# The output linear of the mixer: two of its four pairs as one unit of seven products, with another order of fetches and small work

## The reference, cut to what matters

```python
merged = jax.nn.sigmoid(ga) * (ya @ w_proj_a[l]) + jax.nn.sigmoid(gb) * (yb @ w_proj_b[l])
h = h + gt2[:, None, :] * (merged @ w_out[l])

u = modulate(rmsnorm(h, g_ff2[l]), sh3, sc3)
h = h + FFN_RES * gt3[:, None, :] * swiglu(u, w2_gate[l], w2_up[l], w2_down[l])
```

## Time and profile before

| what | us |
|---|---|
| median of 3 runs (lowest to highest) | 1180.81 (1180.71 to 1181.24) |
| the profiled execution | 1179.22 |
| its span in the trace | 1177.4 |
| TensorE (PE) busy in it | 1164.3 |
| VectorE (DVE) busy | 737.2 |
| ScalarE (ACT) busy | 352.1 |
| GpSimd (POOL) busy | 86.2 |

### The profile page before, as it was taken

One profiled execution on the slowest core, in us unless ns is written; L12 is line 12 of the kernel. 1 busy time (PEld: TensorE's weight loads), 2 busy tenths in 40 slices (PEclk: granted clock), 3 DMA queues, 4 the chain that ended last, 5 costly groups with the idle time before them and its releaser, 6 DMA issues.

```text
span 1177.4 us, 21319 instructions
## 1 busy us (share of the span) xinstructions
PE 1164.3 (99%) x8862; PEld 1076.8 (91%) x8862; DVE 737.2 (63%) x1658; ACT 352.1 (30%) x996; POOL 86.2 (7%) x104
## 2 busy tenths in 40 slices
PE   9999999999999999999999999999999999999997
PEld 7889999998878999999999999988888998888887
DVE  4558888675148866982898888567845231167632
ACT  2111210232124555212321210245333431056542
POOL 0000000200011000022000000310004010001111
PEclk9999999999999999999999999999999999999999
DMA  9969949762655457676599759574524643642311
GB/s 344 366 217 321 315 154 313 290 245 90 219 180 187 150 214 259 236 264 231 185 342 304 235 201 294 193 260 171 146 61 144 215 144 114 187 136 73 117 63 36
DMA packets 164272, 241.78 MB, mean 205 GB/s; under 512 B 14033, under 2 KB 112559, under 8 KB 164176
## 3 DMA queue, kind: packets, MB, share of 16 engines
q1 hardware_dynamic: 156256, 230.45, 57.9%
q10 hardware_dynamic: 6784, 5.74, 1.7%
q0 software_dynamic: 1136, 4.22, 1.1%
HBM read 236.82 MB, written 4.62 MB: 205 GB/s over the span
## 4 chain that ended last, share of the span: by engine, by line
PE 91%; DVE 5%; DMA 2%; ACT 1%; issue 1%; POOL 0%; DVEq 0%; ACTq 0%
PE ps L189 89%; PE ps L192 2%; DVE arena L198 2%; DMA slots<-in_w_proj_a 1%; DVE x L198 1%; DMA slots<-in_w_proj_b 1%; ACT U L195 1%; DVE slots L207 1%; ACT tmps L195 0%; DVE arena L204 0%; DVE rstd L216 0%; DVE tmps L204 0%; DVE slots L198 0%; DVE tmps L198 0%; POOL arena L198 0%
## 5 line engine op out<-in xcount | busy, mean ns | idle before, releaser
L189 PE MATMUL ps<-U,slots 128*128 128x128 f32 (+2 forms) x2800 | 478.7, 330 | 0.0
L189 PEld LDWEIGHTS ps<-U,slots 128*128 128x128 f32 (+1 forms) x2800 | 419.7, 190 | 40.7 <-issue 4.7
L189 PE MATMUL ps<-arena,slots 128*128 128x128 f32 (+1 forms) x1776 | 237.6, 294 | 0.0
L189 PEld LDWEIGHTS ps<-arena,slots 128*128 128x128 f32 x1776 | 225.3, 192 | 8.6 <-issue 0.4
L195 ACT ACTIVATE tmps<-ps 128x256 f32<-128x256 f32 (+2 forms) x151 | 57.4, 383 | 343.4 <-PE ps L189 319.4
L207 DVE CUSTOM_DVE_ANT_0 arena<-arena,tmpA 128x1024 f32<-128x1024 f32 x96 | 118.2, 1275 | 19.3 <-DMA arena<-in_w_adaT 19.1
L195 ACT ACTIVATE arena<-ps 128x256 f32<-128x256 f32 (+3 forms) x150 | 59.5, 416 | 155.9 <-PE ps L189 152.1
L189 PE MATMUL ps<-arena 128*128 128x128 f32 (+7 forms) x940 | 101.9, 287 | 0.9 <-DVE arena L198 0.9
L189 PEld LDWEIGHTS ps<-arena 128*128 128x128 f32 (+2 forms) x940 | 92.4, 181 | 9.8 <-issue 4.2
L189 PE MATMUL ps<-ABT,arena 128*128 128x128 f32 (+5 forms) x752 | 81.9, 271 | 0.0
L189 PEld LDWEIGHTS ps<-ABT,arena 128*128 128x128 f32 (+3 forms) x752 | 72.5, 174 | 0.8 <-issue 0.8
(11 more groups left out here) (199 smaller groups left out, 1140.6 us busy)
## 6 DMA issues: line engine op xcount, KB each, us to landing
slots<-in_w_in SPq DMA_DIRECT2D x14, 2048.0 KB, 10.3
slots<-in_w_down SPq DMA_DIRECT2D x16, 1408.0 KB, 9.8
slots<-in_w_gate SPq DMA_DIRECT2D x18, 1024.0 KB, 8.0
slots<-in_w_up SPq DMA_DIRECT2D x18, 1024.0 KB, 10.8
arena<-in_w_adaT SPq DMA_DIRECT2D x36, 512.0 KB, 6.1
arena<-in_ada_w1T SPq DMA_DIRECT2D x24, 512.0 KB, 7.5
slots<-in_a_in_w SPq DMA_DIRECT2D x6, 2048.0 KB, 9.8
slots<-in_b_in_w SPq DMA_DIRECT2D x12, 1024.0 KB, 5.4
```

What stands on the lines that cost most here:

```text
L189: return Nothing() if self.e is None else self.e.matmul(*a, **k)
```

## The change

The output linear's block 0 (pairs 0 and 1) becomes the fourteenth entry of `U7`, with `GA` as its source, and stands between the first halves of pairs 2 and 3. Each "ada" transfer is fetched behind the two blocks of weights that it stood ahead of, and wo 0 ahead of ada 17. The pieces of ada are moved to other j by a table, the last four behind the loop: two behind the first residual of pair 2, two behind that of pair 3, and mod 17 behind those. The third sums t3 of ("pa", 0) and ("pb", 0) go behind `v_s7` of their source. The residual of block 0 is taken from SBUF in four instructions.

```diff
             for n, g in (("ga", 13), ("gb", 14), ("op", 15), ("pa", 16), ("pb", 17)):
-                fetch("ada", g)
                 fetch(n, 0)
                 fetch(n, 1)
-            fetch("wo", 0)
+                if n == "pb":
+                    fetch("wo", 0)
+                fetch("ada", g)
             fetch("wo", 1)
...
-        U7 = [("xm", 1), ("va", 0), ("va", 1)] + [(n, b) for n in ("ga", "gb", "op", "pa", "pb") for b in range(2)]
+        U7 = [("xm", 1), ("va", 0), ("va", 1)] + [(n, b) for n in ("ga", "gb", "op", "pa", "pb") for b in range(2)] + [("wo", 0)]
-        OF7 = {"pa": "ya", "pb": "hc"}
+        OF7 = {"pa": "ya", "pb": "hc", "wo": "mg"}
...
+            elif n == "wo":
+                x = two(arena[:, 11296:12320])
...
+        def source_in(tag, k):
+
+            return act.at("ya out", k // 2) if tag == "ya" else dve.at("yb", k) if tag == "hc" else pool.at("mg", k // 4, 0)
...
-            mg = lambda k, half: pool.at("mg", k // 4, 1)
-            for pair in range(4):
-                t_linear(e, "wo", pair, GA, mg, half=0 if pair >= 2 else None, side=pair == 0)
-                if pair == 1:
-                    for x in free_of(S3) + free_of(X2):
-                        e.wait_ge(*x)
+            mg = lambda k, half: pool.at("mg", k // 4, half)
+            t_linear(e, "wo", 2, GA, mg, half=0)
+            t_u7_first(e, 13)
+            t_u7_second(e, 13)
+            t_linear(e, "wo", 3, GA, mg, half=0)
+            for x in free_of(S3) + free_of(X2):
+                e.wait_ge(*x)
             t_linear(e, "wo", 2, GA, mg, half=1)
             t_sums_half(e, "n3", 0)
             t_linear(e, "wo", 3, GA, mg, half=1)
...
+        PIECES = {18: (0, 1), 19: (1, 2), 20: (2, 3), 21: (3, 4), 22: (4, 5), 23: (5, 6), 24: (6, 8), 25: (8, 10), 26: (10, 12),
+                  28: (12, 13), 29: (13, 14), 30: (14, 16)}
...
+                    if j in (28, 32):
+                        v_t7_3(e, U7.index(("pa" if j == 28 else "pb", 0)))
...
-                    elif i < 12 and j != 7:
+                    elif i < 13 and j != 7:
                         if j != 3:
                             v_t7_12(e, i + 1)
-                        v_t7_3(e, i + 1)
+                        if j not in (27, 31):
+                            v_t7_3(e, i + 1)
...
-                if j >= 18 and j % 4 == 2 and j < 35:
-                    v_ada_mods(e, 13 + (j - 18) // 4)
-                if 14 <= j < 34:
-                    v_ada_blocks(e, 13, 2 * (j - 14), 2 * (j - 14) + 2)
+                n0, n1 = PIECES.get(j, (0, 0))
+                if n0 and n0 % 4 == 0:
+                    v_ada_mods(e, 12 + n0 // 4)
+                v_ada_blocks(e, 13, 2 * n0, 2 * n1)
+            v_ada_mods(e, 16)
             v_gated_b(e, 1, 1)
             e.tensor_scalar(sm[:, 128:136], mods[:, 40:48], 0.5, None, ALU.mult).then_inc(*dve.up())
             e.wait_ge(*dve.now())
-            for pair in range(4):
-                v_residual(e, "wo", pair, sm[:, 128:136], "n2", 0 if pair >= 2 else None)
+            v_s7(e, "mg", GA, [pool.at("mg", 1, 1)], ("pb", 1))
+            v_t7_4(e, 13)
+            v_residual(e, "wo", 2, sm[:, 128:136], "n2", 0)
+            v_ada_blocks(e, 13, 32, 36)
+            v_u7_c1(e, 13)
+            v_u7_c22(e, 13)
+            done7(e, "wo", 0)
+            for c in range(4):
+                e.wait_ge(*h_in("n2", c, 1))
+                e.stt(H[:, c, :], arena[:, 11296 + T * c:11296 + T * c + T], sm[:, 128 + c:129 + c], H[:, c, :], ALU.mult, ALU.add).then_inc(*dve.up())
+                for half in range(2):
+                    dve.mark("res", "wo", c, half)
+            v_residual(e, "wo", 3, sm[:, 128:136], "n2", 0)
+            v_ada_blocks(e, 13, 36, 40)
+            v_ada_mods(e, 17)
             v_scale(e, "n3", V("g_ff2"), 56)
             v_root(e, "n3", 0)
             v_normed(e, "n3", 0)
...
-            for i in (11, 12):
+            for i in (11, 12, 13):
                 s_u7_out(e, i - 1)
                 s_u7_s1(e, i)
                 s_u7_mid(e, i)
                 s_u7_u3(e, i)
-            s_u7_out(e, 12)
+            s_u7_out(e, 13)
             s_squares_early(e, "n3")
```

More of the change, by code:

```diff
@@ L1465, in source7 @@
         def source7(u):
-            return {"ya": YA, "hc": HC, "u": U}[OF7.get(u[0], "u")]
+            return {"ya": YA, "hc": HC, "mg": GA, "u": U}[OF7.get(u[0], "u")]
+        def source_in(tag, k):
+            return act.at("ya out", k // 2) if tag == "ya" else dve.at("yb", k) if tag == "hc" else pool.at("mg", k // 4, 0)
         def t_u7_first(e, i):
@@ L1473, in t_u7_first @@
             for k in range(4 if tag != "u" else 0):
-                e.wait_ge(*(act.at("ya out", k // 2) if tag == "ya" else dve.at("yb", k)))
+                e.wait_ge(*source_in(tag, k))
             _, free = r.open("7", "A", *u)
@@ L1523, in first7 @@
                 return [pe.at("da mix", 7)]
+            if n == "wo":
+                return [dve.at("ga", 1)]
             return []
```

## The result

The changed kernel takes 1185.0 us (median of 20 runs, 1182.78 to 1186.33) against 1180.93 for the kernel before in the same comparison: ratio 1.0032, interval 1.0026 to 1.0038, so 3.1 to 4.5 us slower. The profiled execution took 1182.94 us with a span of 1181.1, 3.7 over the span of 1177.4 before. The time lies in the stated range and on the stated side. The likeliest case said +2.8 us (1183.6, with a range of its own from 1182.5 to 1184.8; the measured 1185.0 lies just above it), and the rival with the fallen clock +4.0 (1184.8). Executions of one kernel, the kernel before too, start in ways that lie up to 2.5 us apart: the first row of 24 matmul records on `U` stands at 16.89 in the trace before, at 17.00 in the changed kernel's and at 18.92 in that of e3, far ahead of every edit.

What follows compares the result with a forecast made beforehand. TensorE, busy 1164.3 of 1177.4 us, was taken to bound the kernel. A tail longer by 3.67 us and -0.87 upstream gave +2.8 on the median 1180.81: 1183.6 us, range 1181.0 to 1185.7.

Steps and rivals of the forecast that it cites:

- The likeliest case: Whole kernel: tail +3.67 and upstream -0.87 give +2.8 us, 1183.6, own range 1182.5 to 1184.8; chance 0.60.
- the rival with the fallen clock: TensorE's clock halves behind the new 4.4 us hole before n3's sum: +4.0 us, 1184.8; chance 0.20.
- Part 3: GpSimd's squares of n3 queue behind its wait for the later mod 17: a TensorE hole of 4.4 us.
- Part 1: Output linear's pairs 0 and 1 on TensorE: seven products replace two pairs, gaining 1.26 us.
- S: Moment when the last product of ("pb", 1) ends on TensorE, predicted at 527.05; later times count from it.
- the merge hole: TensorE waits in pair 2's first half for GpSimd's third merge: 0.50 us, or 0.35 if the merge is uncontended.
- Part 2: New order behind ("pb", 1): pair 2's first half wants mg(k >= 4) early, opening a hole of 0.50 us.
- Part 4: Upstream fetch order and pieces: two old TensorE holes close, one opens at the flips; -0.87 us in sum.
- The flips: TensorE's flips near 467 wait for X2 banks, since delayed pieces hold up ScalarE's tanh: new hole of 0.89 us.
- The two old holes: TensorE's waits for VectorE's sums at 478.39 and 505.50, 1.23 and 0.53 us; both were to close.
- The sum: Total for the kernel: +3.67 in the tail and -0.87 upstream, +2.8 us, 1183.6.
- The other side: Rival: GpSimd's queue does not bind before n3's sum, so no hole there: -1.6 us, 1179.2; chance 0.07.

Runs made afterwards that it cites:

- e3: Changed kernel with fetches, pieces and third sums as before, leaving only the seven-product unit and the order of pairs; ratio 0.9996 to the kernel before.
- e2: Kernel before with only ada 17 fetched late, its four pieces and mod 17 put behind residuals of pairs 0 and 3; ratio 1.0045.
- e5: Changed kernel with the last two pieces and mod 17 moved behind pair 2's first residual; 1179.3 us against 1181.05, ratio 0.9991.
- e1: Changed kernel with GpSimd's squares of n3 ahead of its wait for mod 17 and the copy of c; 1181.4 us against 1181.29, ratio 0.9999.
- e8: Changed kernel with all four last pieces behind pair 2's first residual, only mod 17's small addition behind pair 3's; ratio 1.0005.
- e7: Changed kernel with three of the last four pieces behind pair 2's first residual, one with mod 17 behind pair 3's; ratio 1.0023.

## Why the prediction was right, and where its sizes were off

The mechanism of Part 3 was right and decided the sign; it is shown by e2 (alone it makes the hole), e5 and e1 (without it the loss is gone) and e8 (the mark, not the work, sets it). Step by step, with distances between starts of rows:

- **Part 1, seven products: -1.26.** From S (525.90) to the moment at which the sum was wanted (540.82 + 80 records of 0.1117 = 549.76) are 23.86 us; less the merge hole, 23.34, against 24.53 before: -1.19. Right.
- **Part 2, the merge hole: +0.50.** 24 records behind 524.11 end at 526.79, the next starts at 527.31: 0.52. Right; the row's 0.36 is less, since it counts from the modelled end of the last matmul.
- **Part 4, upstream: -0.87.** Measured -1.27. The flips cost 1.01 (from 459.73 to 474.56 are 14.83 us, before 13.82), a little over the 0.89 (the two times it was taken from, 468.03 and 467.19, are 0.84 apart); ScalarE's tanh waited as said, 1.03. The two old holes gave back 1.38 and 0.68 where their rows say 1.23 and 0.53, and the rest of the 0.40 us is in the restart of the stream behind a hole. An idle figure is too small by 0.15 where the stream before it is matmuls.
- **Part 3, the wait: sum at S + 28.2.** Measured S + 28.5. The copy's issue took 0.57, the squares 3.96; nothing stood behind the issue. Right. The 0.3 us more is the step from mod 17 to the issue, 0.32 us, for which the sum had no term (its terms for mod 17 give S + 23.4, rounded up to 23.5; measured S + 23.6).
- **The sum: +2.8.** At the first sum +2.81, or +2.7 counted from the common row. Part 4 was 0.40 too small a gain, Part 3 0.3 too small a loss: that they nearly cancel is luck.
- **The clock.** The likeliest case left it at full, and that is the step that failed: "no row shows a hole of that size" was taken as a reason for one chance in five. The trace of the kernel before had a view that speaks against it, at its end, where TensorE has no more work:

```profile
1171.18 0.49 PE L189 MATMUL ps<-tmps,cst 128*128 128x128 f32 x2 [0.62 <-ACT tmps L195]
```

```profile
1174.00:1175.00 1.00, 0.00 (x0) 0.00 (x0) 0.38 (x1) 0.00 (x0) 0.00 (x0) 0.97 0.24 73
1175.00:1176.00 1.00, 0.00 (x0) 0.00 (x0) 0.00 (x0) 0.00 (x0) 0.00 (x0) 0.50 1.01 287
```

  TensorE's last matmul ends at 1171.67 and the clock is at half from about 1174.9: 3.3 us of idleness were enough there, and the forecast had 4.4. So the clock was down at half not only near 8 to 11 us, as the prediction has it, and the rival deserved more than 0.20. Its price was near in both parts: 1.5 less 0.3 reckoned, 1.50 less 0.52 measured, 0.98 in all, and its +4.0 is nearer to the 4.1 between the medians than the likeliest case's +2.8. How long the clock was down in the executions that weren't profiled was not seen, so the last 0.4 us between the trace's 3.7 and the medians' 4.1 is left open.
- **The other side** was priced wrong. With the queue's wait out of the way (e1) the time was to be 1.6 us under the kernel before; it was the same. The price left out that two pieces and the squares would then run side by side. The place of the pieces costs 1.8 us once the queue's wait is gone (e1 against e5).

## What to carry to other kernels

A mark that is moved moves everything that is queued behind a wait for it, also in programs that the edit doesn't touch: here one in-order wait on GpSimd cost 4.5 us of TensorE, more than twice what both intended gains brought (1.2 and some 0.5 to 0.7). Put small work of VectorE where it waits for TensorE anyway, and not beside GpSimd's instructions. The four holes of 2.1 us and more cost 1.0 to 1.9 us beyond their length, and would have cost half a microsecond more without the old wait behind them, so a new wait is to be priced with the clock. Look for the price of an idle TensorE in the whole trace, its end too, before saying that no row shows it.

## What was not expected of the hardware

- The clock fell behind a hole of 2.08 us (e8) and stayed at full behind one of 1.83 (e1). It fell during the hole in the changed kernel and in e2, and 1.1 to 1.2 us after its end in e7 and e8, with TensorE at work again.
- The price did not follow the length of the hole. It was half of the time that TensorE worked while the clock was at half, and so hung on when the clock fell and on how long it stayed down:

| kernel | hole | at half | TensorE at work in it | sum and half linear longer by | distance of the two sums longer by |
|---|---|---|---|---|---|
| e8 | 2.08 | 554.5 to 557.9 | 3.4 | 1.72 | 1.2 |
| e7 | 3.34 | 556.7 to 560.1 | 3.4 | 1.72 | 1.2 |
| changed | 4.48 | 553.9 to 557.35 | 3.0 | 1.50 | 1.0 |
| e2 | 4.49 | 555.9 to 562.8 | 4.8 | 2.39 | 1.9 |

  The last column is less by 0.5, the old wait at the second sum that fell away. These are one execution each; e1's hole of 1.83, without a fall, has 0.10 and 0.1 in the last two columns.
- Instructions of GpSimd and VectorE side by side: 0.73 became 1.59, 0.45 became 1.44, and a piece of 1.22 became 1.74 (e1).
